# The product of gate and up kept in PSUM, and a chunk's low part formed in one GpSimd instruction, in a two-block transformer kernel

## The reference

```
def swiglu(x, w_gate, w_up, w_down):
    return (jax.nn.silu(x @ w_gate) * (x @ w_up)) @ w_down      # D_FF = 2816

def first_block(x, ...):
    x = layer_norm(alpha * x + 0.5 * swiglu(x, ffn 0), ...)
    x = layer_norm(alpha * x + hybrid_mixer(x, ...), ...)       # three kinds of attention, gates
    x = layer_norm(alpha * x + 0.5 * swiglu(x, ffn 1), ...)

def second_block(x, p, ...):
    u = rmsnorm(h, ...)                                          # gated delta rule and sparse attention
    h = h + rmsnorm(mixed, ...)
    f = rmsnorm(h, ...) @ w_up
    f = causal_dwconv(f, conv_ffn) + conv_ffn_b                  # 3 taps
    f_gate, f_val = jnp.split(f, 2, axis=-1)
    f = (jax.nn.gelu(f_gate) * f_val) @ w_down
    h = h + rmsnorm(f, ...)
    e = (p @ w_ple) * jax.nn.sigmoid(h @ w_ple_gate)
    h = h + rmsnorm(e, ...)
```

## Time and profile before

| | |
|---|---|
| median of 3 runs | 1125.18 us (1123.74 to 1125.71) |
| span of the profiled execution, first to last instruction | 1122.6 us |
| granted TensorE clock, mean of the core | 0.998 |
| TensorE busy | 1094.1 us, 97%, 8110 instructions |
| GpSimd busy | 902.3 us, 80%, 695 instructions |
| ScalarE busy | 621.2 us, 55% |
| VectorE busy | 495.1 us, 44%, 904 instructions |
| moved from memory | 189 MB, mean 170 GB/s |

### The profile page before, as it was taken

One profiled execution on the slowest core, in us unless ns is written; L12 is line 12 of the kernel. 1 busy time (PEld: TensorE's weight loads), 2 busy tenths in 40 slices (PEclk: granted clock), 3 DMA queues, 4 the chain that ended last, 5 costly groups with the idle time before them and its releaser, 6 DMA issues.

```text
span 1122.6 us, 22288 instructions
## 1 busy us (share of the span) xinstructions
PE 1094.1 (97%) x8110; PEld 1023.2 (91%) x8110; DVE 495.1 (44%) x904; ACT 621.2 (55%) x1002; POOL 902.3 (80%) x695
## 2 busy tenths in 40 slices
PE   8999999999999999999999999999999999999997
PEld 7999998999998998999999899889999798999985
DVE  4422113202456554421126655774766256454463
ACT  4444444654667866544443775555666565555564
POOL 6999996898664596999999589577355898999985
PEclk9999999999999999999999999999999999999999
DMA  7866665666342454766665466335233565666652
GB/s 244 282 204 193 187 195 165 206 222 192 115 131 78 130 184 139 230 202 198 192 182 181 135 193 188 118 116 159 65 94 127 183 202 172 180 197 187 189 184 77
DMA packets 52774, 191.29 MB, mean 170 GB/s; under 512 B 5856, under 2 KB 6112, under 8 KB 52320
## 3 DMA queue, kind: packets, MB, share of 16 engines
q1 hardware_dynamic: 50688, 182.47, 52.6%
q10 hardware_dynamic: 2016, 7.81, 2.1%
HBM read 189.21 MB, written 1.05 MB: 169 GB/s over the span
## 4 chain that ended last, share of the span: by engine, by line
POOL 51%; issue 27%; PE 19%; ACT 1%; POOLq 1%; DVE 1%; DMA 1%; SPq 0%; DVEq 0%; ACTq 0%
POOL weights_low L533 51%; PE banks L575 10%; PE acc L575 8%; DMA ring<-in_stream 1%; POOLq L539 0%; ACT weights_high L1440 0%; POOLq L530 0%; ACT tmp L1686 0%; ACT tmp L1956 0%; PE acc L749 0%; PE banks L766 0%; DVE act_buf L2016 0%; DVE res L2162 0%; POOL stat L547 0%; DVE xs L2174 0%
## 5 line engine op out<-in xcount | busy, mean ns | idle before, releaser
L533 POOL TENSOR_TENSOR weights_low<-ring,weights_high 128x512 fp32r<-128x512 f32 x686 | 899.2, 1345 | 208.7 <-ACT weights_high L1440 206.5
L1440 ACT CAST weights_high<-ring 128x1024 fp32r<-128x1024 f32 x343 | 356.1, 1047 | 216.4 <-PE banks L575 132.0
L575 PE MATMUL banks<-xT_high,weights_high 128*128 128x256 f32 x1264 | 351.5, 278 | 1.2 <-POOL weights_low L533 1.1
L575 PE MATMUL banks<-xT_low,weights_high 128*128 128x256 f32 x1264 | 350.3, 277 | 0.0
L575 PE MATMUL banks<-xT_high,weights_low 128*128 128x256 f32 x1264 | 350.3, 277 | 0.0
L575 PEld LDWEIGHTS banks<-xT_high,weights_high 128*128 128x128 f32 x1264 | 237.4, 188 | 4.2 <-issue 1.5
L575 PEld LDWEIGHTS banks<-xT_low,weights_high 128*128 128x128 f32 x1264 | 237.7, 188 | 2.3
L575 PEld LDWEIGHTS banks<-xT_high,weights_low 128*128 128x128 f32 x1264 | 237.9, 188 | 0.0
L1991 DVE TENSOR_TENSOR hf<-act_buf,banks 128x256 f32<-128x256 f32 x40 | 16.8, 421 | 225.2 <-ACT act_buf L1466 211.0
L575 PE MATMUL acc<-xT_high,weights_high 128*128 128x256 f32 x408 | 108.8, 287 | 1.8 <-ACT xT_high L1539 1.0
L575 PE MATMUL acc<-weights_high,hT_high 128*128 128x512 f32 x264 | 104.0, 394 | 2.2 <-issue 1.6
(11 more groups left out here) (362 smaller groups left out, 1577.5 us busy)
## 6 DMA issues: line engine op xcount, KB each, us to landing
ring<-in_stream SPq DMA_DIRECT2D x343, 512.0 KB, 3.7
rows<-in_big_rows ACTq DMA_DIRECT2D x3, 1024.0 KB, 8.2
rows<-in_big_rows ACTq DMA_DIRECT2D x3, 512.0 KB, 4.0
cst<-in_consts ACTq DMA_DIRECT2D x3, 470.5 KB, 4.8
xs<-in_x_tm ACTq DMA_DIRECT2D x2, 512.0 KB, 7.3
out<-xs SPq DMA_DIRECT2D x4, 256.0 KB, 2.1
gates<-in_x_fm SPq DMA_DIRECT2D x2, 256.0 KB, 4.2
ring<-in_stream SPq DMA_DIRECT2D x2, 256.0 KB, 4.3
```

The costliest lines, as they stand in the source:

```text
L533: last = nc.gpsimd.tensor_tensor(wlo[:, slot, hs], ring[:, slot, hs], whi[:, slot, hs].bitcast(F32), ALU.subtract)
L575: ins = nc.tensor.matmul(o, lhsT, rhs, start=start, stop=stop, **kw)
L1440: nc.scalar.copy(whi[:, ch % RING, :], ring[:, ch % RING, :]).then_inc(S["hi_ready"], 1)
```

## The change

Three things. (1) In all three feed-forwards the product of activation and up is written back to its PSUM tile ([T:2T]) instead of the SBUF buffer `hf`; the cast (L1998) then reads PSUM, and the subtraction (L2000) reads the PSUM tile and `hT_high`. In FFN2 ScalarE's gelu is written into the tile's [0:T] instead of the SBUF buffer `gel`, so that the product reads PSUM and `act_buf`. (2) GpSimd forms a chunk's low part with one instruction of 1024 columns. (3) As the tiles of f = 0 and 1 now hold the products until they are split, the first `down` waits for `hidden` of both.

```diff
-        hf = sb("hf", [2, T], in_ffn)
+        sb("fill_act", [2 * T], in_ffn)
-        gel = sb("gel", [2, T], in_ffn)
...
             def low(slot, value):
                 pool.wait_ge(S["hi_ready"], value)
-                for half in range(2):
-                    hs = slice(512 * half, 512 * half + 512)
-                    last = nc.gpsimd.tensor_tensor(wlo[:, slot, hs], ring[:, slot, hs], whi[:, slot, hs].bitcast(F32), ALU.subtract)
-                last.then_inc(S["lo_ready"], 1)
+                nc.gpsimd.tensor_tensor(wlo[:, slot, :], ring[:, slot, :], whi[:, slot, :].bitcast(F32), ALU.subtract
+                                        ).then_inc(S["lo_ready"], 1)
...
-                    pe.wait_ge(S["hidden"], NF * n + f + 1 + GROUP * it)
-                    if very_first:
-                        pe.wait_ge(S["h_made"], NF * n + 2)
+                    pe.wait_ge(S["hidden"], NF * n + f + (2 if very_first else 1) + GROUP * it)
...
-                nc.scalar.activation(gel[:, f % 2, :], act_buf[:, f % 2, 0:T], ACT.Gelu_apprx_tanh).then_inc(S["act_done"], 1)
+                nc.scalar.activation(ffn_tile(2, f, it)[:, 0:T], act_buf[:, f % 2, 0:T], ACT.Gelu_apprx_tanh).then_inc(S["act_done"], 1)
...
-                v.tensor_tensor(hf[:, f % 2, :], act_buf[:, f % 2, 0:T], ffn_tile(n, f, it)[:, T:2 * T], ALU.mult
-                                ).then_inc(S["h_made"], 1)
-                split_hidden(n, f, it)
+                product = ffn_tile(n, f, it)[:, T:2 * T]
+                v.tensor_tensor(product, act_buf[:, f % 2, 0:T], product, ALU.mult).then_inc(S["h_made"], 1)
+                split_hidden(n, f, it, product)
...
-                v.tensor_copy(hT[0][:, f % GROUP, :], hf[:, f % 2, :]).then_inc(S["h_high"], 1)
+                v.tensor_copy(hT[0][:, f % GROUP, :], product).then_inc(S["h_high"], 1)
                 dve.wait_ge(S["h_high"], value)
-                v.tensor_tensor(hT[1][:, f % GROUP, :], hf[:, f % 2, :], hT[0][:, f % GROUP, :].bitcast(F32), ALU.subtract
+                v.tensor_tensor(hT[1][:, f % GROUP, :], product, hT[0][:, f % GROUP, :].bitcast(F32), ALU.subtract
                                 ).then_inc(S["hidden"], 1)
...
-                v.tensor_tensor(hf[:, f % 2, :], gel[:, f % 2, :], act_buf[:, f % 2, T:2 * T], ALU.mult
-                                ).then_inc(S["h_made"], 1)
-                split_hidden(2, f, it)
+                tile = ffn_tile(2, f, it)
+                v.tensor_tensor(tile[:, T:2 * T], tile[:, 0:T], act_buf[:, f % 2, T:2 * T], ALU.mult).then_inc(S["h_made"], 1)
+                split_hidden(2, f, it, tile[:, T:2 * T])
```

More of the change, by code:

```diff
@@ L1990, in hidden, with split_hidden @@
                     dve.wait_ge(S["down_done"], (NF - 3) * n + f - GROUP + 1 + GROUP * it)
-                v.tensor_tensor(hf[:, f % 2, :], act_buf[:, f % 2, 0:T], ffn_tile(n, f, it)[:, T:2 * T], ALU.mult
-                                ).then_inc(S["h_made"], 1)
-                split_hidden(n, f, it)
-            def split_hidden(n, f, it):
+                product = ffn_tile(n, f, it)[:, T:2 * T]
+                v.tensor_tensor(product, act_buf[:, f % 2, 0:T], product, ALU.mult).then_inc(S["h_made"], 1)
+                split_hidden(n, f, it, product)
+            def split_hidden(n, f, it, product):
                 value = NF * n + f + 1 + GROUP * it
                 dve.wait_ge(S["h_made"], value)
-                v.tensor_copy(hT[0][:, f % GROUP, :], hf[:, f % 2, :]).then_inc(S["h_high"], 1)
+                v.tensor_copy(hT[0][:, f % GROUP, :], product).then_inc(S["h_high"], 1)
                 dve.wait_ge(S["h_high"], value)
-                v.tensor_tensor(hT[1][:, f % GROUP, :], hf[:, f % 2, :], hT[0][:, f % GROUP, :].bitcast(F32), ALU.subtract
+                v.tensor_tensor(hT[1][:, f % GROUP, :], product, hT[0][:, f % GROUP, :].bitcast(F32), ALU.subtract
                                 ).then_inc(S["hidden"], 1)
```

## The result

The changed kernel takes 1137.94 us (median of 4 runs, 1136.91 to 1139.35); the kernel before, measured beside it, took 1125.0 (median of 4). The ratio is 1.0115, 95% interval [1.0102, 1.0128]: slower by 1.2%, 12.9 us, where 9.5 were forecast. The span of the profiled execution is 1136.6 against 1122.6, 14.0 more.

What follows compares the result with a forecast made beforehand. TensorE was taken to bound the feed-forwards' bodies, so only its stops elsewhere count. Losses of 13.8 less gains of 3.4 gave +10.4, after slack +9.5; 1122.6 + 2.6 + 9.5 = 1134.7 us, range 1123 to 1140.

Steps and rivals of the forecast that it cites:

- rival (d): Wherever turns are on the path: one wide instruction saves nothing, a turn lasts 0.16 us more; 1138.7 us, chance 0.08.
- What bounds the kernel: Feed-forward bodies: TensorE needs 2.76 us a chunk, GpSimd 2.54, so time changes only where TensorE stands still.
- Part 1: Feed-forwards, product in PSUM: 45 us less of VectorE, worth -1.7 at FFN2's first down, -0.6 and -0.3 at ends.
- The ends: Ends of FFN1 and FFN2: TensorE no longer waits for a low part that `hT_low` held up, -0.6 and -0.3 us.
- The length of the wide instruction: GpSimd's low part: one 1024-column instruction takes 2.38 us, between 2.34 and 2.54, gaining 0.16 us a chunk.
- The turns: Port shared by VectorE and GpSimd: locked for a whole instruction, so chained turns grow from 1.4 to about 2.5 us.
- rival (b): At the shared port: turns of 1.45 us stay whatever GpSimd's width, losses 0, gains stay; 1121.8 us, chance 0.14.
- the seven places: Start +2.0, layer norms +2.1, stick-breaking +1.7, first compression +3.6, delta rule +1.2, second compression +2.6, mask product +0.6: +13.8 us.
- the second compression: Seven GpSimd instructions from 750.41: four turns lost, partly covered by TensorE's own work, +2.6 us.
- 800: A mask product of the sparse attention at 800: a loss of +0.6 us.
- (a): At the listed places: the lock holds, but half of the losses fall into slack; +3.5, 1128.7 us, chance 0.24.
- (c): At the listed places: a quarter of the losses is left and cancels the gains; 1125.2 us, chance 0.12.

Runs made afterwards that it cites:

- e3: Changed kernel with GpSimd's 1024 columns only in the feed-forwards' bodies, 512 twice everywhere else; 1122.33 us, ratio 0.9975 to the kernel before.
- e1: Changed kernel with GpSimd back at two instructions of 512 columns, so only the product in PSUM; 1121.53 us, ratio 0.9968 to the kernel before.
- e2: Kernel before with only GpSimd's single 1024-column instruction added, without the product in PSUM; 1141.96 us, ratio 1.0149 to the kernel before.
- e4: Changed kernel with 512 columns twice in the feed-forwards' bodies and 256 four times everywhere else; 1137.85 us, ratio 1.0108 to the kernel before.
- e10: e1 with 256 columns four times only for the 16 chunks formed at about 660 to 700 us; 1127.63 us, ratio 1.0027 to the kernel before.
- e5: Changed kernel with 512 columns twice in the first block outside its feed-forward bodies; 1132.20 us, ratio 1.0059 to the kernel before.
- e6: Changed kernel with 512 columns twice for the chunks between FFN1 and FFN2; 1128.98 us, ratio 1.0033 to the kernel before.

## Why the prediction was right

The forecast was 1134.7 in a range of 1123 to 1140; it came out at 1137.9, slower, by the mechanism of the forecast. The nearest number of all was rival (d)'s, 1138.7, by a mechanism that the traces refute; the forecast's own number was 3.2 too low.

**What bounds the kernel** held: the feed-forwards' bodies gave and cost nothing in any of the kernels (the flat stretches, e3), and the chain's 51% for GpSimd was no bound.

**Part 1** held for FFN2's first down: forecast -1.7, measured -1.7, and -1.5 in e1. The ends, forecast at -0.6 and -0.3, came to -0.8 and -0.4 (and -0.3 at the norm), but e2 has the same steps without part 1, so the forecast's reason for them, that `hT_low` held GpSimd up, is not shown. e1 puts all of part 1 at 3.3 us.

**The length of the wide instruction**: 2.38 was taken between 2.34 and 2.54; one that stands alone is shown with 2.35, and in a row they start 2.36 apart. Rival (d) is refuted. The straight line through the figure of the Trainium skill (GPSIMD Engine Reference, section 3.1), an estimate of 2.35, came nearer than the forecast's 2.38.

**The turns**: held, which refutes rival (b); contending instructions of a chain last 2.6 where they lasted 1.4 to 1.5, and e4's 0.96 gives a third point. It is what the Trainium skill, SBUF — State Buffer, section "SBUF: two separate sides", says of the shared port pair; e4 and e10 show a case that its words don't cover, an instruction that is passed over at two dozen boundaries. Of the seven places, five came within 0.1 us; the second compression was 0.4 too large; and at 800 the instruction took 1.1 us longer, as forecast, but TensorE lost nothing by it, while 0.5 came from another one at 825: that this makes up for it is luck. e5 and e6 give the places back where they were put, which refutes rivals (a) and (c): nearly all the losses reached TensorE.

**What was too small** is the sum, 9.5 against 12.9 in the medians and 14.0 in the profiles. At the places that the forecast names the steps sum to 9.4, where its terms gave 10.4 and 9.5 after the tenth taken off for slack. So that number came out, though not by slack between the places as the forecast says: the second compression gave 0.4 less, the place at 800 nothing, and the gains were 0.4 larger. The shortfall lies wholly in what the list doesn't have, of three kinds.

- *Turns that were not listed* (721, 825 and 859: +1.0, +0.5, +1.0). The first and the last are of instructions that waited in the first half of a chunk before as well, so that the forecast's own rule gives each +1.11; they took 1.08 and 0.97 longer. The rule was right and the search for places incomplete: one of them showed only 0.42 us, which doesn't look like a wait until it is set beside the 0.16 and 0.17 of its neighbours with 4 and 8 columns. Ahead of the one at 825 a VectorE instruction of 1024 columns takes 3.33 us where it took 1.30; that it is the cause is read from the order of the instructions, not tested.
- *The clock* (+0.8 and +1.6, of which 0.9 is taken back). TensorE can come out of a wait at half speed. The forecast has no term for it. Behind the wait of 4.77 us this follows from the change, by the five traces above; behind the one of 2.13 us it is not shown. Over all runs the change does cost clock: the mean granted clock is 0.992 to 0.995 in the four runs of the changed kernel and 0.995 to 0.999 in the 37 of the kernel before, 0.003 apart on the mean, which over 1138 us is at most 3.4 us (an estimate from these two numbers).
- *The two spacings* (+0.8). In one stretch matmuls of 256 columns start 0.118 instead of 0.113 us apart at a granted clock of 1.00. Both spacings occur in every kernel here, at changing places, and what sets them is open; that this one fell on the changed kernel's profile may be chance.

The 2.6 us that the forecast took as lying around the profiled span did no harm, for it only leads back to the median. The runs show 1.9 there (1138.5 against a span of 1136.6); the rest was the profiled execution of before being quicker than its median.

## What to carry to other kernels

When two engines take turns at a port, the length of one instruction is the other's waiting time: merging instructions on the engine that has time to spare saved 0.14 us each here, and is paid for by every instruction of the other engine that stands on the critical path. Take the contention away first (an operand in PSUM), merge only where none is left, and cut finer only at chains that the busiest engine waits for, looking in the trace for an instruction that doesn't get its turn. When listing the places, take every contending instruction on the path, also one that shows only a short wait. Price a wait of 4 to 5 us on TensorE with a half-speed stretch behind it, and one of 2 us with the chance of one; and before explaining such a stretch by a change, look whether it also comes and goes without it.

## What was not expected of the hardware

- A VectorE instruction of 8 columns with two SBUF inputs stood for 16.57 and 16.55 us while GpSimd's 256-column instructions followed each other, in two kernels; with 512 columns it got the next boundary, 0.40 us. A third one, of 1024 columns, was passed over for 4.51 us.
- The granted clock fell to its lower level, for 3 us or twice that, at all five unfilled waits of TensorE of 4.26 to 5.47 us and behind 9 of the 21 of 1.90 to 2.13 us; where the long one was filled with matmuls it stayed at 1.00.
- The two spacings of equal matmuls, 0.113 and 0.118 us, at the same granted clock.
